# Sharing one load of second-half query weights between chunks 0 and 1, keeping the pool weights, and asking chunks 2 and 3 one pass earlier

## The chip, the cores and the metric

The kernel runs on one core of a Trainium2 chip. The metric is the time of one execution on the device, in microseconds (us). Before the change it is 2883.5 us, the median of three runs (2882.57 to 2884.82).

## What is computed

The input x holds 512 tokens of width 1024. Two layers are applied to it. Layer 0 mixes tokens with four moving averages (the "pool"), layer 1 with an attention over a compressed key-value memory. After the mixer each layer has a retrieval stage (PEER), which is most of the work:

```python
q = (h @ w_q).reshape(B, S, 8, 2, 128)             # 8 heads, two query halves each
s = einsum('bshpc,hpnc->bshpn', q, sub_keys)       # against 128 keys per half
top_s, top_i = top_k(s, 16)                        # 16 best keys of each half
best_s, pos = top_k(all 16 x 16 sums, 16)          # 16 best pairs of each head
gate = softmax(best_s)
a = einsum('tkd,td->tk', u[idx], h)                # 128 expert rows per token
x = x + einsum('tk,tkd->td', gate * gelu(a), v[idx])
```

A last stage adds x + sigmoid(norm(x) @ ple_wg) * (p @ ple_wp). All data are float32. A token wants 8 heads x 16 = 128 experts in each layer, and the rows u and v of an expert stand side by side in memory (8 KB).

## The kernel before

**Chunks, passes, gathers.** The 512 tokens are four chunks of 128. A chunk in a layer is a pair g (0 to 3 in layer 0, 4 to 7 in layer 1). Pass g runs over the 128 experts of pair g. For each expert k one indirect DMA, a gather, fetches 128 rows of 8 KB (1 MB) into one of 9 slots. There are 1024 gathers. The queue of POOL (GpSimd) issues them (line 582), and each waits until the addition of the gather nine places before has freed its slot. DVE takes the dot product of u and h (line 1648), ACT makes gelu, weight and a diagonal matrix (lines 1150 to 1158), and then either PE adds v into the accumulator in PSUM by two products with that diagonal matrix (line 933), or DVE adds it into X (line 1639). `on_dve(n)` decides which: `ADDS_ON_DVE` gives the number of additions on DVE in each pass, spread evenly over it. PE can run ahead by no more than the 5 diagonal matrices.

**Everything else happens between gathers.** A stage is a generator on each engine and is cut into parts. `STEPS[g]` lists the stages of pass g in order, and `placed_parts(g)` sets the gather before which each part begins: parts have shares (`PARTS`), and they are laid out in proportion over gathers 2 to 110 of the pass, as if there were at least 165 shares (`PACE`). In pass 0 they are laid out from gather 13. `BESIDE[g]` holds the rank stages that run beside them. Each engine works in order, so a part that waits holds up all additions and dot products behind it.

**The stages that matter here.**
- `pool` (a norm, a transposing product, a scaling into `TP`, a product with `pool_w`, a scaling into SD, an addition into X), for chunk 0 at the start and for chunks 1 to 3 in pass 0.
- `fnorm` normalises up to two chunks and puts their transposes into the halves of `TT`.
- `asks0` and `asks1` are the queries and key scores of heads 0 to 3 and 4 to 7. Each uses four pieces of `w_q` of 1 MB (pieces 0 to 3, and 4 to 7), and for each piece and chunk DVE finds the 16 best of two rows of scores (`top16`).
- `rank0` and `rank1` make expert numbers and gates of four heads. In pass 0 the first heads have stages of their own, `rank_a`, `rank_b`, `rank_c`. A gather whose k begins a new group of heads waits for their numbers.

**Which pass does what.** Chunk 0 is asked at the start (`asks0`) and in pass 0 (`asks1`). Chunk 1 has `asks0` in pass 0 and `asks1` in pass 1. Chunks 2 and 3 go together: `asks0` in pass 1, `asks1` in pass 2, in front of the embedding of chunks 0 and 1 and the keys and values of layer 1.

**Where weights stand.** SP's queue loads all pieces, in the order of `PIECES`. A piece goes to a ring of two buffers (`RING`) as soon as the piece two places before it has been used. The five pieces of the start (`pool_w` and `w_q` 0 to 3) lie in gather slots 4 to 8. `KEPT` pieces go into the key-value memory KV, which layer 0 doesn't need: `w_q` 0 to 3, loaded once for chunk 1 and used again for chunks 2 and 3. That load waits until the pool stage is over, since the pool works in KV:

```python
if where == "KV" and not there and i == 0:
    next_ffn = NC + 2 if name == "ple_wg" else g0
    sp.wait_ge(x_ready, before("x_ready", "fnorm", next_ffn))
```

Of the kernel before, what the change touches and what calls it, by code (L numbers as in the profile page):

```python
# [25 lines left out]
P = 128  # L26
S, D, DEPTH = 512, 1024, 2
NC = S // P
# [25 lines left out]
ADDS_ON_DVE = (32, 28, 32, 44, 32, 42, 26, 64)  # L54
# [46 lines left out]
RANKS = {"rank0": (0, 4), "rank1": (4, 4), "rank_a": (0, 1), "rank_b": (1, 1), "rank_c": (2, 2)}  # L101


def ranks_of(g):

    names = ("rank_a", "rank_b", "rank_c", "rank1") if g == 0 else ("rank0", "rank1")
    return {RANKS[name][0] * TOPK: name for name in names}

# [29 lines left out]
def attention(g0):  # L138
# [52 lines left out]
    "rank_c": lambda g, n: [5, 5],  # L191
    "residual": lambda g, n: [2, 0],
# [57 lines left out]
PLACE = {g0 + i: i for s, g0, n in SCHEDULE if s == "fnorm" for i in range(n)}  # L250
# [19 lines left out]
FIRST_SLOT = SLOTS - FIRST_PIECES  # L270

KEPT = [("wq", (1, 2)), ("ple_wg", (4, 6, 7))]


def homes():


    found, ringed, first = [], [], {}
    for (name, g0, i), n in PIECES.items():
        kept = [(k, groups) for k, (kept_name, groups) in enumerate(KEPT)  # L280
                if name == kept_name and g0 in groups and i < 4]
        if n < FIRST_PIECES:
            found.append(("slot", FIRST_SLOT + n, 0, None, False))
        elif kept:
            k, groups = kept[0]
            found.append(("KV", i, k, None, g0 != groups[0]))
        else:
# [13 lines left out]
         (8, "main", "asks0", 5), (10, "beside", "rank_c", 0), (13, "beside", "rank_c", 1)]  # L301


def placed_parts(g):

    placed, done = [[] for _ in range(KSEL)], 0
# [5 lines left out]
    total = max(PACE * last, sum(sum(PARTS[st[0]](*st[1:])) for st in STEPS[g]))  # L312
    for st in STEPS[g]:
        for part, share in enumerate(PARTS[st[0]](*st[1:])):
            placed[begin + int(done * (last - begin) / total)].append(("main", st, part))
            done += share
    beside = [(st, part) for st in BESIDE[g] if st[0] not in ("rank_b", "rank_c") for part in range(len(PARTS[st[0]](*st[1:])))]
    for i, (st, part) in enumerate(beside):
        first = 2 + max(u for u in range(KSEL) if any(s[0] == "asks1" for _, s, _ in placed[u]))
        at = first + 8 * i if i < 2 else first + 18 + (i - 2) * (last - 10 - first - 18) // 3  # L320
        placed[at].append(("beside", st, part))
# [55 lines left out]
def trunk(nc, consts, pools, gcols, gains, positions, x, pT, uv, weights, keys, out):  # L377
    ctx = ExitStack()
    with ctx:
# [79 lines left out]
        TP = TT[:, :, P:2 * P]  # L459
# [62 lines left out]
        def _(sp):  # L522
# [5 lines left out]
            for (name, g0, i), n in PIECES.items():  # L528
# [38 lines left out]
        def _(pool):  # L567

            nc.gpsimd.memset(rooted[:], 1.0).then_inc(one_ready, 1)
            for g in range(PAIRS):  # L570
                for k in range(KSEL):
# [3 lines left out]
                    if n < SLOTS:  # L575
                        if s >= FIRST_SLOT:
                            pool.wait_ge(weights_used, s - FIRST_SLOT + 1)
# [11 lines left out]
        def _(pe):  # L589
# [35 lines left out]
            def pool_stage(g0, n):  # L625
                for i in range(n):
# [22 lines left out]
                    for wnd in range(len(WINDOWS)):  # L649
                        for k in range(2):  # L650
                            last = nc.tensor.matmul(M[:, wnd * GW:(wnd + 1) * GW], TP[:, 2 * wnd + k, :],
# [20 lines left out]
            def asks_stage(half, g0, n):  # L672

                stage, width = f"asks{half}", n * P

# [1080 lines left out]
```

## Time and profile before

| What | Value |
|---|---|
| Median of three runs | 2883.5 us |
| The profiled execution | 2884.08 us |
| Its span, first to last instruction | 2882.3 us |
| Mean granted TensorE clock | 0.912 of full |
| PE / DVE / ACT / POOL busy | 79% / 74% / 37% / 45% |
| Moved by DMA | 1175.37 MB, mean 408 GB/s |
| Gathers' share of it | 1073.81 MB |

The span is what the profile covers. 1.8 us of the execution lie around it. Busy shares are of the span. A matmul's end is modelled, so a busy PE is not a PE at its limit. The DMA figures come from the packets of the core's 16 DMA engines.

### The profile page before, as it was taken

Reading aid. Unit: us, or ns where it says so; the run is one execution under the profiler, and the core shown is the slowest. Engines: PE = TensorE matmul, PEld = TensorE weight load, DVE = VectorE, ACT = ScalarE, POOL = GpSimd, SP = SyncE. Lnnn points to the kernel's source line nnn. Section 1 sums busy time; section 2 is a strip of 40 time slices with the busy share of each in tenths; the row PEclk is TensorE's granted clock in tenths of the full one; section 3 lists DMA queues with packets and bytes.
Section 4 is the critical chain, followed back from the end, with each engine's and each line's share of the span. In section 5 each row is a group of like instructions: output and inputs, shape, how many; then the busy total and the mean of one; then the engine's idle time right before and its main releaser. Section 6 shows DMA issues by size and latency. Waiting matters only on the chain.

```text
span 2882.3 us, 23329 instructions
## 1 busy us (share of the span) xinstructions
PE 2265.8 (79%) x6572; PEld 1170.4 (41%) x6572; DVE 2143.5 (74%) x4489; ACT 1072.4 (37%) x3181; POOL 1282.7 (45%) x1029
## 2 busy tenths in 40 slices
PE   6787667976978987888687898799967788666555
PEld 4444234522534553455253455346624433222112
DVE  6888768875797667757979766686696977677776
ACT  2443324333334333632323434364332334333222
POOL 2353543544434544533543443454444334555552
PEclk9899988988999998999898999999988999887877
DMA  9999999999999999999999999999999999999995
GB/s 363 420 399 420 419 421 401 417 420 420 419 408 412 380 420 420 419 420 420 408 420 384 416 374 419 421 419 420 420 398 420 419 420 420 420 420 420 420 421 216
DMA packets 164786, 1175.37 MB, mean 408 GB/s; under 512 B 18480, under 2 KB 19888, under 8 KB 23600
## 3 DMA queue, kind: packets, MB, share of 16 engines
q0 software_dynamic: 147456, 1073.81, 90.3%
q1 hardware_dynamic: 16624, 98.24, 8.4%
q10 hardware_dynamic: 576, 1.84, 0.2%
q8 instruction: 52, 0.85, 0.1%
q14 instruction: 78, 0.64, 0.1%
HBM read 1171.71 MB, written 2.10 MB: 407 GB/s over the span
## 4 chain that ended last, share of the span: by engine, by line
PE 36%; DMA 35%; DVE 18%; ACT 5%; issue 4%; POOL 2%; DVEq 0%; SPq 0%; ACTq 0%; POOLq 0%
DMA slot<-in_uv,idx 35%; PE acc L933 18%; DVE slot L1648 6%; DVE X L1639 3%; PE B L687 3%; PE B L605 3%; PE M L605 2%; POOL slot L582 2%; PE M L875 2%; PE M L687 1%; PE B L875 1%; ACT diag L1158 1%; DVE SD L1275 1%; DVE top_u L1280 1%; ACT A L948 1%
## 5 line engine op out<-in xcount | busy, mean ns | idle before, releaser
L933 PE MATMUL acc<-slot,diag 128*128 128x512 f32 x2904 | 1550.7, 673 | 580.9 <-ACT diag L1158 580.1
L582 POOL DMA_INDIRECT slot<-in_uv,idx x1024 | 1282.4, 1252 | 1555.3 <-PE acc L933 1076.4
L1648 DVE CUSTOM_DVE_ANT_0 slot<-slot,HP 128x1024 f32<-128x1024 f32 x1024 | 1243.3, 1221 | 564.2 <-DMA slot<-in_uv,idx 554.4
L933 PEld LDWEIGHTS acc<-slot,diag 128*128 128x128 f32 x2904 | 571.5, 210 | 1413.0 <-ACT diag L1158 853.7
L1150 ACT ACTIVATE act_a<-a 128x1 f32<-128x1 f32 x1024 | 206.6, 202 | 1616.7 <-DVE a L1648 1615.7
L1639 DVE SCALAR_TENSOR_TENSOR X<-slot,w,X 128x1024 f32<-128x1024 f32 x297 | 380.7, 1282 | 33.4 <-ACT w L1152 33.2
L1152 ACT ACTIVATE w<-act_a,gate 128x1 f32<-128x1 f32 x1024 | 301.5, 294 | 33.2
L1158 ACT ACTIVATE diag<-cst,w 128x128 f32<-128x128 f32 x726 | 291.7, 402 | 23.8
L687 PE MATMUL B<-TT,w 128*128 128x256 f32 (+1 forms) x448 | 88.8, 354 | 0.0
L687 PE MATMUL M<-TT,w 128*128 128x256 f32 (+1 forms) x448 | 88.3, 352 | 0.0
L687 PEld LDWEIGHTS B<-TT,w 128*128 128x128 f32 x448 | 78.3, 196 | 20.7 <-issue 13.1
L687 PEld LDWEIGHTS M<-TT,w 128*128 128x128 f32 x448 | 77.3, 194 | 19.4 <-issue 12.0
L1648 DVE DVE_READ_ACCUMULATOR2_ANT a<- 128x1 f32 x1024 | 84.3, 82 | 0.0
L1150 ACT ACT_TABLE_LOAD x56 | 71.8, 1283 | 12.3 <-DVE a L1648 9.4
L605 PE MATMUL M<-w,TT 128*128 128x256 f32 x272 | 61.6, 379 | 0.0
L605 PE MATMUL B<-w,TT 128*128 128x256 f32 x272 | 61.6, 379 | 0.0
L605 PEld LDWEIGHTS M<-w,TT 128*128 128x128 f32 x272 | 51.7, 190 | 14.7 <-issue 8.6
L605 PEld LDWEIGHTS B<-w,TT 128*128 128x128 f32 x272 | 51.7, 190 | 10.9 <-issue 4.3
L1273 DVE MAX8 top<-T 128x8 f32<-128x128 f32 x128 | 37.6, 294 | 15.9 <-PE T L702 15.7
L875 PE MATMUL M<-KV,TT 128*128 128x512 f32 x96 | 43.7, 603 | 0.0
L1278 DVE MAX8 top<-SD 128x8 f32<-128x128 f32 x128 | 37.8, 295 | 4.4
L702 PEld LDWEIGHTS T<-TU,A 128*128 128x128 f32 x256 | 34.4, 191 | 16.2 <-issue 14.6
(203 smaller groups left out, 1553.5 us busy)
## 6 DMA issues: line engine op xcount, KB each, us to landing
w<-in_wq SPq DMA_DIRECT2D x28, 1024.0 KB, 9.1
slot<-in_uv,idx POOLq DMA_INDIRECT x1024, 16.9
w<-in_ple_wg SPq DMA_DIRECT2D x8, 1024.0 KB, 9.1
w<-in_w_o SPq DMA_DIRECT2D x8, 1024.0 KB, 9.1
w<-in_w_dq SPq DMA_DIRECT2D x6, 1024.0 KB, 6.9
w<-in_w_uq_nope SPq DMA_DIRECT2D x8, 768.0 KB, 8.6
w<-in_ple_wp SPq DMA_DIRECT2D x5, 1024.0 KB, 14.2
slot<-in_wq SPq DMA_DIRECT2D x4, 1024.0 KB, 15.2
```

What stands on the lines that cost most here:

```text
L582: nc.gpsimd.indirect_dma_start(out=slot[s][:], out_offset=None, in_=uv[g // NC], in_offset=bass.IndirectOffsetOnAxis(ap=idx[:, g % HPB, k: ...
L605: last = nc.tensor.matmul(dst, lhsT[:, k, i * P:(i + 1) * P], wp[:, k * cols:(k + 1) * cols], start=(k == 0), stop=(k == kb - 1))
L687: last = nc.tensor.matmul(dst[:, e * 512:e * 512 + width], wp[:, k * 256 + e * P:k * 256 + (e + 1) * P], TT[:, k, 0:width], start=(k == 0) ...
L875: last = nc.tensor.matmul(MB[ch][:, half * 512:half * 512 + 512], TT[:, k0 + k, ch * P:(ch + 1) * P], wp[:, k * 512:k * 512 + 512], start= ...
L933: last = nc.tensor.matmul(acc[:, half * 512:half * 512 + 512], diag[adds_on_pe(n) % DIAGS][:], slot[s][:, D + half * 512:D + half * 512 + ...
L1150: nc.scalar.activation(act_a[:, s:s + 1], a[:, s:s + 1], ACT.Gelu_apprx_tanh).then_inc(gelued, 1)
L1152: nc.scalar.activation(w[:, s:s + 1], act_a[:, s:s + 1], ACT.Copy, scale=gate[:, g % HPB, k:k + 1]).then_inc(weighted, 1)
L1158: nc.scalar.activation(diag[adds_on_pe(n) % DIAGS][:], ident, ACT.Copy, scale=w[:, s:s + 1]).then_inc(diag_ready, 1)
L1273: step(nc.vector.max(tops[:, 0:8], values))
L1278: step(nc.vector.max(tops[:, 8:16], left))
L1639: nc.vector.scalar_tensor_tensor(Xc, slot[s][:, D:2 * D], w[:, s:s + 1], Xc, ALU.mult, ALU.add).then_inc(dve_added, 1)
L1648: nc.vector.tensor_tensor_reduce(out=slot[s][:, 0:D], in0=slot[s][:, 0:D], in1=HP[:, g % HPB, :], scale=1.0, scalar=0.0, op0=ALU.mult, op1 ...
```

## The change

Three things are changed.

1. `asks1` of chunks 0 and 1 is one stage in pass 0, `asks1 (0, 2)`, which loads `w_q` 4 to 7 once for both. For it chunk 1 goes through `pool` and `fnorm` first, so that both transposes stand in `TT`; `place_of` fixes which half. Chunk 0's ranking of heads 4 to 7 is cut in two (`rank_d`, `rank_e`). The parts of these stages are laid out over gathers 13 to 55 (`ASKED`), and the rest of the pass's parts over 55 to 110.
2. `pool_w` goes to the fourth quarter of KV and is loaded once for all chunks. `TP`, into which the pool writes, moves from `TT` to SD.
3. Chunks 2 and 3 have `asks1` in pass 1, behind their `asks0`. Pass 2 keeps the embedding, the keys and values, and the ranking of chunk 3. `trig` moves from pass 0 to pass 1, and `rank1` of chunk 2 from pass 2 to pass 1.

With it, the additions on DVE are given for each quarter of a pass: 28 in pass 0 (32 before), 22 in pass 1 (28), 43 in pass 2 (32), and as many as before in the others.

```diff
-ADDS_ON_DVE = (32, 28, 32, 44, 32, 42, 26, 64)
+QUARTER = KSEL // 4
+ADDS_ON_DVE = ((4, 4, 9, 11), (7, 5, 5, 5), (10, 6, 11, 11), (11, 11, 11, 11),
+               (8, 8, 8, 8), (10, 11, 10, 11), (7, 6, 7, 6), (16, 16, 16, 16))
...
-    spread, of = ADDS_ON_DVE[g] - DVE_HEAD, KSEL - DVE_HEAD
-    return (k - DVE_HEAD) * spread // of != (k - DVE_HEAD + 1) * spread // of
+    q, j = divmod(k, QUARTER)
+    head = DVE_HEAD if q == 0 else 0
+    spread, of = ADDS_ON_DVE[g][q] - (head if g else 0), QUARTER - head
+    return (j - head) * spread // of != (j - head + 1) * spread // of
...
 STEPS = [
-    (ask_second(0, 1) + stages_of(["pool"], 1, 3) + ask_first(1, 1) +
-     stages_of(["trig"], 0, 1)),
-    residual(0) + ask_second(1, 1) + ask_first(2, 2),
-    residual(1) + ask_second(2, 2) + stages_of(["renorm"], 3, 1) + embed(0, 2) + keys_values(4),
+    (stages_of(["pool", "fnorm"], 1, 1) + ask_second(0, 2) + stages_of(["rank_e"], 0, 1) +
+     stages_of(["pool"], 2, 2) +
+     stages_of(["asks0"], 1, 1) + rank(1, 0)),
+    residual(0) + rank(1, 1) + ask_first(2, 2) + ask_second(2, 2) + rank(2, 1) + stages_of(["trig"], 0, 1),
+    residual(1) + stages_of(["renorm"], 3, 1) + embed(0, 2) + keys_values(4),
...
 BESIDE = [
-    stages_of(["rank_b", "rank_c"], 0, 1) + rank(0, 1),
-    rank(1, 1),
-    rank(2, 1) + rank(3, 0) + rank(3, 1),
+    stages_of(["rank_b", "rank_c", "rank_d"], 0, 1),
+    [],
+    rank(3, 0) + rank(3, 1),
...
-FIRST_SLOT = SLOTS - FIRST_PIECES
-KEPT = [("wq", (1, 2)), ("ple_wg", (4, 6, 7))]
+FIRST_SLOT = SLOTS - FIRST_PIECES + 1
+POOL_HOME = 3
+KEPT = [("pool_w", (0, 1, 2)), ("wq", (1, 2)), ("ple_wg", (4, 6, 7))]
...
+ASKED = 55
...
+    for sts, end, pace in ((STEPS[g][:3], ASKED, 0), (STEPS[g][3:], last, 0)) if g == 0 else ((STEPS[g], last, PACE),):
+        done, total = 0, max(pace * last, sum(sum(PARTS[st[0]](*st[1:])) for st in sts))
...
+        if g == 0:
+            at = (ASKED - 8, ASKED - 5)[i]
+        elif g == 2:
+            at = 20 + i * (last - 30) // 3
...
-        TP = TT[:, :, P:2 * P]
+        SDH = SD[:, :].rearrange("p (a d) -> p a d", a=2)
+        scaled, TP = SDH[:, :, 0:D // 2], SDH[:, :, D // 2:D]
...
-                if where == "KV" and not there and i == 0:
-                    next_ffn = NC + 2 if name == "ple_wg" else g0
-                    sp.wait_ge(x_ready, before("x_ready", "fnorm", next_ffn))
+                if where == "KV" and not there and i == 0 and g0:
+                    free_at = ("fnorm", NC + 2) if name == "ple_wg" else ("asks0", g0)
+                    sp.wait_ge(x_ready, before("x_ready", *free_at))
...
                 stage, width = f"asks{half}", n * P
+                lo = place_of(g0) * P
+                if (half, g0) == (0, 1):
+                    pe.wait_ge(x_ready, before("x_ready", stage, g0))
...
-                                                    TT[:, k, 0:width], start=(k == 0), stop=(k == DB - 1))
+                                                    TT[:, k, lo:lo + width], start=(k == 0), stop=(k == DB - 1))
```

## Rows read from the trace of the kernel before

**Rows 1.** The page: GB/s in 40 slices, and all DMA packets.

```profile
GB/s 363 420 399 420 419 421 401 417 420 420 419 408 412 380 420 420 419 420 420 408 420 384 416 374 419 421 419 420 420 398 420 419 420 420 420 420 420 420 421 216
DMA packets 164786, 1175.37 MB, mean 408 GB/s; under 512 B 18480, under 2 KB 19888, under 8 KB 23600
```

**Rows 2.** Windows: the start, passes 0 to 6, the end; last columns clock, DMA share, GB/s.

```profile
0.00:42.80 42.80, 23.91 (x160) 21.84 (x160) 17.41 (x61) 7.00 (x13) 4.79 (x10) 0.96 0.84 324
42.80:391.60 348.80, 267.91 (x872) 140.33 (x873) 274.22 (x647) 132.66 (x397) 162.70 (x132) 0.91 1.01 416
391.60:726.20 334.60, 261.36 (x718) 129.46 (x717) 252.31 (x581) 119.40 (x380) 154.91 (x129) 0.89 1.01 415
726.20:1101.10 374.90, 327.42 (x979) 180.35 (x978) 277.65 (x608) 140.98 (x407) 166.63 (x129) 0.94 1.00 408
1101.10:1451.60 350.50, 277.55 (x867) 152.55 (x866) 266.29 (x538) 143.31 (x419) 157.47 (x129) 0.93 1.01 417
1451.60:1830.50 378.90, 323.10 (x980) 178.26 (x979) 277.69 (x608) 140.57 (x407) 158.01 (x129) 0.95 0.99 403
1830.50:2182.00 351.50, 300.78 (x1002) 168.26 (x1001) 267.14 (x536) 150.09 (x421) 159.51 (x129) 0.94 1.01 415
2182.00:2530.70 348.70, 274.20 (x659) 124.00 (x657) 260.56 (x574) 129.71 (x391) 150.86 (x129) 0.93 1.01 420
...
2842.00:2882.30 40.30, 22.62 (x49) 9.80 (x48) 21.15 (x33) 12.36 (x28) 0.00 (x0) 0.84 0.14 56
```

**Rows 3.** DMA issues of weights: count, KB each, median us to landing.

```profile
w<-in_wq SPq DMA_DIRECT2D x28, 1024.0 KB, 9.1
...
KV<-in_wq SPq DMA_DIRECT2D x4, 1024.0 KB, 16.1
...
w<-in_pool_w SPq DMA_DIRECT2D x1, 1024.0 KB, 8.9
```

**Rows 4.** Windows in passes 2 and 4, in which DMA falls short.

```profile
920.00:956.00 36.00, 32.94 (x129) 21.65 (x129) 26.74 (x56) 16.59 (x49) 18.90 (x10) 0.95 0.85 326
...
948.00:956.00 8.00, 8.00 (x28) 4.96 (x27) 5.49 (x11) 5.43 (x16) 7.39 (x3) 1.00 0.35 121
...
1664.00:1688.00 24.00, 21.53 (x67) 12.75 (x68) 18.63 (x33) 10.12 (x32) 16.87 (x9) 0.93 0.77 299
```

**Rows 5.** POOL's timeline from 941 us: gathers 335 and 336.

```profile
944.78 9.07 POOL L582 DMA_INDIRECT slot<-in_uv,idx  x1 [1.44 <-PE acc L933]
954.16 0.94 POOL L582 DMA_INDIRECT slot<-in_uv,idx  x1 [0.30 <-issue]
```

**Rows 6.** The page: all gathers of POOL; busy, mean ns, idle before, releaser.

```profile
L582 POOL DMA_INDIRECT slot<-in_uv,idx x1024 | 1282.4, 1252 | 1555.3 <-PE acc L933 1076.4
```

**Rows 7.** DVE's timeline beside it: seven dot products and an addition, first and last.

```profile
943.77 1.20 DVE L1648 CUSTOM_DVE_ANT_0 slot<-slot,HP 128x1024 f32<-128x1024 f32 x1
...
951.83 1.21 DVE L1648 CUSTOM_DVE_ANT_0 slot<-slot,HP 128x1024 f32<-128x1024 f32 x1
```

**Rows 8.** Window of gathers 16 to 39 of pass 2.

```profile
770.00:847.00 77.00, 61.13 (x174) 30.57 (x173) 71.18 (x207) 28.84 (x81) 32.88 (x25) 0.91 1.01 409
```

**Rows 9.** DVE's timeline in pass 2: a top16, a dot, an addition, the next top16.

```profile
796.12 0.28 DVE L1273 MAX8 top<-T 128x8 f32<-128x128 f32 x1
...
797.71 1.21 DVE L1648 CUSTOM_DVE_ANT_0 slot<-slot,HP 128x1024 f32<-128x1024 f32 x1
...
798.84 1.28 DVE L1639 SCALAR_TENSOR_TENSOR X<-slot,w,X 128x1024 f32<-128x1024 f32 x1
800.04 0.29 DVE L1273 MAX8 top<-T 128x8 f32<-128x128 f32 x1
```

**Rows 10.** PE's timeline: half a query piece for two chunks, one addition.

```profile
760.13 3.62 PE L687 MATMUL B<-TT,w 128*128 128x256 f32 x16
763.59 1.88 PE L933 MATMUL acc<-slot,diag 128*128 128x512 f32 x4
```

**Rows 11.** PE's timeline in pass 7: one addition, begun after a wait.

```profile
2684.70 3.66 PE L933 MATMUL acc<-slot,diag 128*128 128x512 f32 x4 [3.00 <-ACT diag L1158]
```

More of the change, by code:

```diff
@@ L191 @@
     "rank_c": lambda g, n: [5, 5],
+    "rank_d": lambda g, n: [5, 5],
+    "rank_e": lambda g, n: [5, 5],
     "residual": lambda g, n: [2, 0],
@@ L248, with place_of, asked_in @@
     t == "latent" for t, _, _ in SCHEDULE[max([0] + [j for j in range(i) if SCHEDULE[j][0] == "asks0"]):i]))]
-PLACE = {g0 + i: i for s, g0, n in SCHEDULE if s == "fnorm" for i in range(n)}
+def place_of(g):
+    return g % GROUP
+def asked_in(half, g):
+    return g if g == 0 or (g == 1 and half == 0) else g - g % GROUP
 def before(name, stage, g0):
@@ L269 @@
 FIRST_PIECES = sum(len(ids) for st in START for _, ids in USES.get(st[0], []))
-FIRST_SLOT = SLOTS - FIRST_PIECES
-KEPT = [("wq", (1, 2)), ("ple_wg", (4, 6, 7))]
+FIRST_SLOT = SLOTS - FIRST_PIECES + 1
+POOL_HOME = 3
+KEPT = [("pool_w", (0, 1, 2)), ("wq", (1, 2)), ("ple_wg", (4, 6, 7))]
 def homes():
-    found, ringed, first = [], [], {}
+    found, ringed, loads = [], [], [0] * 4
     for (name, g0, i), n in PIECES.items():
[L280 to L286, printed above, removed]
+        kept = [groups for kept_name, groups in KEPT if name == kept_name and g0 in groups and i < 4]
+        if kept:
+            home, there = POOL_HOME if name == "pool_w" else i, g0 != kept[0][0]
+            loads[home] += not there
+            found.append(("KV", home, loads[home] - 1, None, there))
+        elif n < FIRST_PIECES:
+            found.append(("slot", FIRST_SLOT + n - 1, 0, None, False))
         else:
@@ L301 @@
          (8, "main", "asks0", 5), (10, "beside", "rank_c", 0), (13, "beside", "rank_c", 1)]
+ASKED = 55
 def placed_parts(g):
-    placed, done = [[] for _ in range(KSEL)], 0
+    placed = [[] for _ in range(KSEL)]
     begin, last = DVE_HEAD - 1, KSEL - 18
@@ L311, in placed_parts @@
             placed[at].append((lane, (name, 0, 1), part))
[L312 to L316, printed above, removed]
+    for sts, end, pace in ((STEPS[g][:3], ASKED, 0), (STEPS[g][3:], last, 0)) if g == 0 else ((STEPS[g], last, PACE),):
+        done, total = 0, max(pace * last, sum(sum(PARTS[st[0]](*st[1:])) for st in sts))
+        for st in sts:
+            for part, share in enumerate(PARTS[st[0]](*st[1:])):
+                placed[begin + int(done * (end - begin) / total)].append(("main", st, part))
+                done += share
+        begin = end
     beside = [(st, part) for st in BESIDE[g] if st[0] not in ("rank_b", "rank_c") for part in range(len(PARTS[st[0]](*st[1:])))]
     for i, (st, part) in enumerate(beside):
-        first = 2 + max(u for u in range(KSEL) if any(s[0] == "asks1" for _, s, _ in placed[u]))
-        at = first + 8 * i if i < 2 else first + 18 + (i - 2) * (last - 10 - first - 18) // 3
+        if g == 0:
+            at = (ASKED - 8, ASKED - 5)[i]
+        elif g == 2:
+            at = 20 + i * (last - 30) // 3
+        else:
+            first = 2 + max(u for u in range(KSEL) if any(s[0] == "asks1" for _, s, _ in placed[u]))
+            at = first + 8 * i if i < 2 else first + 18 + (i - 2) * (last - 10 - first - 18) // 3
         placed[at].append(("beside", st, part))
@@ L576, in _ @@
                         if s >= FIRST_SLOT:
[L577 removed]
+                            pool.wait_ge(weights_used, s - FIRST_SLOT + 2)
                     elif on_dve(n - SLOTS):
@@ L1140, in _ @@
                           rank_c=lambda g, n: rank_stage("rank_c", g, n),
+                          rank_d=lambda g, n: rank_stage("rank_d", g, n),
+                          rank_e=lambda g, n: rank_stage("rank_e", g, n),
                           latent=latent_stage, keys=keys_stage, dq=dq_stage, uq=uq_stage, uqp=uqp_stage,
@@ L1282, in asks_stage @@
             def asks_stage(half, g0, n):
-                stage = f"asks{half}"
+                stage, first = f"asks{half}", place_of(g0)
                 yield
@@ L1625, in _ @@
                           rank_c=lambda g, n: rank_stage("rank_c", g, n),
+                          rank_d=lambda g, n: rank_stage("rank_d", g, n),
+                          rank_e=lambda g, n: rank_stage("rank_e", g, n),
                           latent=latent_stage, dq=dq_stage, uqp=uqp_stage, heads=heads_stage, wo=wo_stage,
```

35 lines of the change are left out of this document (22 added, 13 removed).

## The prediction

> **What bounds the kernel now.** I read the page first. In 27 of the 40 slices DMA moves 419 to 421 GB/s, and it never moves more [rows 1]. Over a whole pass it can hold that: pass 6 shows 420 [rows 2]. A gather is 1.0486 MB, so at this rate one costs 2.50 us, and the 1175.37 MB [rows 1] cost 2798.5 us of the span's 2882.3. The other 83.8 us are time in which DMA was short. POOL's waits for a freed slot [rows 6] fit: the ring of 9 slots is full most of the time.
>
> The second view is the table by pass, to find where DMA is short. I take a stretch's loss as its length times (420 - its GB/s) / 420 [rows 2]. The start loses 42.8 x 96/420 = 9.8 us, and the end 40.3 x 364/420 = 34.9. Passes 0 to 6 lose 3.3, 4.0, 10.7, 2.5, 15.3, 4.2 and 0 us. So bytes set the time, and a local stall counts only where it outlasts the ring. The third view is the stretch of pass 2 that loses most. From 920 to 956 us it loses 36 x 94/420 = 8.1 us, of which the last 8 us alone lose 5.7 [rows 4]. There one gather sat on POOL for 9.07 us, against a mean of 1.25, and the next followed at once with no wait for a slot [rows 5, 6]. In the same time DVE ran seven dot products and an addition without a gap [rows 7].
>
> **The bytes.** The change takes away five pieces of 1 MB. `asks1 (1, 1)` no longer loads `w_q` 4 to 7, and `pool_w` is loaded once instead of twice (its load into the ring [rows 3] goes). The first `w_q` pieces for chunks 1 to 3 are kept in KV before and after, and the ring then holds two pieces of `asks1 (2, 2)` from pass 0 on, and gets the other two in pass 1 instead of pass 2. The keys are loaded as often as before. 5 x 1.0486 = 5.24 MB at 420 GB/s are **-12.5 us**. That term has no upper bound beyond itself: if all five loads now filled time in which DMA was short anyway, it would be 0, and at most the 18.0 us lost in passes 0 to 2 could hide some of it. I take all of it, as the loads fall mostly in stretches at 420.
>
> **Pass 2.** It loses `asks1 (2, 2)` and `rank1` of chunk 2. The shares laid out over 108 gathers fall from 252 to 194. The latent stage begins at gather 44 instead of 59, and its part after the `w_dkv` products follows 6 gathers later instead of 4. DVE's burst between gathers 16 and 39 goes: there it was busy 71.2 of 77 us, and the stretch lost 77 x 11/420 = 2.0 us [rows 8]. The run of seven dots that goes with the long gather came from a backlog that DVE had built at the latent stage. With the parts wider apart the backlog shrinks. I take the loss of pass 2 from 10.7 to 3.0 us, **-7.7**, the level of passes 0 and 3 [rows 2]. The ends are -10.7 (nothing left) and 0 (all stalls return in new places). DVE gets 11 more additions (43 for 32), 11 x 1.20 = 13 us [rows 9], less than the 16 top16 (25 us) and the ranking (13) that leave.
>
> **Pass 0.** DVE's prices are from one stretch: a top16 796.12 to 797.71, 1.59 us; a dot 1.13; an addition 1.20 [rows 9]. A ranking of two heads I estimate at two top16 (3.2), four operations over 512 elements at half a dot each (2.4) and 2 us of small ones, 7.6 us. DVE's work is heaviest from gather 43 to 62 after the change: 20 dots 22.6, 3 additions 3.6, 12 top16 for heads 5 to 7 of two chunks 19.1, `rank_d` and `rank_e` 15.2, the next pool's norm 0.7, together 61 us. DMA brings 20 gathers in 50 us, and no weights fall there. So DVE falls 11 us behind. What the ring can take: 9 slots x 2.50 = 22.5 us from one issue to the next of a slot, less the 9.1 us of a lone piece to landing [rows 3], less some 4.5 us from dot to free slot (1.1 dot, about 1 on ACT, 1.7 to 2 for the addition), leaves about 9 us. So 2 us are lost. PE in the same stretch, gathers 26 to 55: `asks1 (0, 2)` is four pieces of two halves, 8 x 3.46 = 27.7 us [rows 10], and 3.6 for scores, an estimate. 26 additions on PE (28 of 32 a quarter) at 1.71 us are 45. That is 76 us against 75 of gathers and 5 of weights, so PE is full but doesn't fall behind. It saves little elsewhere. The three pools stay, one before the queries and two behind. The load of `w_q` 0 to 3 waits for the last pool addition (gather 77), and `asks0 (1, 1)` begins at 79, 5 us later. A lone piece takes 9.1 us [rows 3], so PE waits 4 us with its additions queued behind it, and ACT stops after 5 diagonal matrices. DVE goes on. DMA is full with those very loads, and 4 us are inside the ring's 9: price 0; were the ring already late, 4. `rank_d` ends at gather 55, whose slot gather 64 needs: no wait. Pass 0 goes from 3.3 to 5.3 us lost, **+2**. The ends are -3.3 and +11 (the whole backlog shows).
>
> **Pass 1.** The shares rise from 127 (laid out as 165) to 202. From gather 88 to 111 DVE has 24 dots 27.1, 4 additions 4.8, 8 top16 12.7, a ranking of four heads 13 and `trig` 5, 63 us against 60. PE from 21 to 54 has 31 us of queries and scores and 28 additions, 48: 79 us against 82. Both fit narrowly. I take 4.0 to 5.0, **+1**, between -4 and +7. SP's queue, once past `w_q` 7 of chunk 2, waits for `renorm`, now at gather 3 of pass 2. `gates` needs its first piece at 12, 9 gathers or 22 us later, against 9.1 for a load: 0.
>
> **Pass 4 and the rest.** Only the spread of additions changes. In the first quarter of pass 4 DVE has 8 instead of 9 or 10, beside the same burst as in pass 2. That saves 1 to 2 us of a loss of 15.3. I take **-1.5**, between -8 (the long gather of 1664 to 1688 us [rows 4] goes too) and +3.
>
> **The sum.** -12.5 - 7.7 + 2 + 1 - 1.5 = -18.7 us. The profiled execution took 2884.1 (span 2882.3 and 1.8 around it), so it would take 2865.4; the median before is 0.6 lower. I predict **2865 us**.
>
> **A rule weighed.** The long gather [rows 5] beside an unbroken run of DVE operations with two inputs in SBUF [rows 7] looks like POOL being kept out. The Trainium skill, "SBUF — State Buffer", section "Who interferes with whom", says that such a DVE operation contends with GpSimd instructions that read SBUF, and infers that descriptor generation isn't held by it. By that page the 9.07 us belong to POOL alone and would stay at 2871 us in all; by the rows they come with the run of dots, and go when it is broken. No run here separates the two yet.
>
> **Rivals.**
> - *The long gather stays.* It occurs at gather 79 of pass 2 and, with the same loss, of pass 4 [rows 4], 256 gathers apart. If it belongs to the gather's number or to any backlog at `latent`, 5.7 us of pass 2's gain are missing: 2871. For it: the same place twice. Against: both passes have the same order of work, so the same run of dots. Chance 0.18.
> - *The new bursts in passes 0 and 1 cost what pass 2 gives back.* DVE's 11 us and PE's full stretch show in whole: +11 and +7 instead of +3, 2880. For it: pass 4 lost 15.3 with much the same burst. Against: the same burst in pass 2 lost 2.0. Chance 0.10.
> - *More stalls go.* The long gather of pass 4 goes too and pass 2 is clean: 2856. Chance 0.10.
> - *Slower: PE at its lower clock in pass 0.* PE has 76 us of work at full clock in gathers 26 to 55. At the lower level (1.2 GHz) an addition takes 3.66 us instead of 1.88 [rows 10, 11], twice as long. If a share f of this work runs so, PE falls 76(1 + f) - 80 us behind, and what is over 9 is lost. It eats the gain of 19 from f = 0.42. Pass 0 shows a granted clock of 0.91 [rows 2], that is 0.18 of its time at the lower level, and the lower level followed PE's idle time; here PE is never idle. Chance 0.03, 2887.
> - *The loads are hidden anyway*, and only the bytes' time moves into idle DMA: about 2880 with the rest. In the chance of the second rival.
>
> **Chances and range.** The forecast has 0.59, 2860 to 2869. The range takes in the bounds of passes 0 to 2 and of pass 4: 2854 to 2877. It leaves out the slow end and most of the second rival. 0.2% is 5.8 us, about what a measurement of this kernel tells from no change: below 2877.7 is faster. Faster has 0.91, within 0.2% 0.06 (half of the second rival), slower 0.03.
>
> **What would show it.** Bytes: 1170.1 MB, with 24 + 4 loads of `w_q` by ring and slots, one of `pool_w`. Pass 2: GB/s near 417, no gather over 2 us on POOL, length near 362 us (374.9, less two `w_q` pieces or 5.0, less 7.7). Pass 1: about 331 us (two pieces fewer, +1). Pass 0: about 348 (one piece fewer, +2). The window of gathers 43 to 70 of pass 0 shows 400 to 415 GB/s. The forecast is wrong if DMA moves under 412 in pass 0 or 1, or if POOL has a long gather in any of the first three passes.

## The result and the profile after

The change makes the kernel slower: 2890.6 us (median of 12 runs, 2887.4 to 2895.3) against 2883.8 us before (12 runs, 2882.1 to 2885.3). The ratio is 1.0024, with a 95% interval of 1.0016 to 1.0032. The forecast was 2865 us, with a range of 2854 to 2877. The profiled execution has a span of 2888.1 us, 5.8 more than before.

The page of the changed kernel, its GB/s in 40 slices and its packets, answers to [rows 1].

```profile
GB/s 371 387 378 379 419 420 411 399 419 386 420 419 382 420 419 420 419 420 420 405 420 386 416 376 420 420 420 419 420 404 420 419 420 416 420 420 420 420 420 216
...
DMA packets 164065, 1170.11 MB, mean 405 GB/s; under 512 B 18400, under 2 KB 19808, under 8 KB 23520
```

The bytes are as forecast: 1170.1 MB, with 24 loads of `w_q` into the ring and one of `pool_w`. But the mean rate fell from 408 to 405 GB/s, and slices 2 to 4 (72 to 289 us, pass 0) show 378 to 387 where the kernel before had 399 to 420. The table by pass answers to [rows 2]: the start, passes 0 to 5.

```profile
0.00:41.30 41.30, 22.33 (x160) 20.76 (x160) 17.43 (x62) 7.00 (x13) 4.80 (x10) 0.92 0.86 336
41.30:403.50 362.20, 281.85 (x880) 151.13 (x880) 282.33 (x707) 136.75 (x401) 163.49 (x132) 0.91 0.98 397
403.50:738.60 335.10, 274.12 (x760) 140.35 (x760) 272.36 (x709) 127.39 (x392) 149.99 (x129) 0.93 1.00 406
738.60:1107.80 369.20, 298.56 (x801) 151.23 (x802) 249.98 (x437) 134.04 (x394) 165.42 (x129) 0.90 1.00 412
1107.80:1457.70 349.90, 281.97 (x859) 155.05 (x858) 265.82 (x538) 143.22 (x419) 155.94 (x128) 0.90 1.01 417
1457.70:1837.10 379.40, 327.23 (x985) 181.08 (x984) 277.80 (x609) 140.79 (x407) 162.53 (x129) 0.94 0.99 404
1837.10:2188.10 351.00, 300.11 (x996) 167.34 (x995) 267.56 (x536) 149.58 (x421) 165.95 (x128) 0.93 1.01 417
```

By the same formula, length times (420 - GB/s) / 420, the losses are:

| Pass | Lost before, us | Forecast | Lost after | Length before, forecast, after |
|---|---|---|---|---|
| 0 | 3.3 | 5.3 | 19.8 | 348.8, 348, 362.2 |
| 1 | 4.0 | 5.0 | 11.2 | 334.6, 331, 335.1 |
| 2 | 10.7 | 3.0 | 7.0 | 374.9, 362, 369.2 |
| 4 | 15.3 | 13.8 | 14.5 | 378.9, -, 379.4 |

Passes 0 and 1 lose 23.7 us more, the start and passes 2, 4 and 5 some 7.7 less, and the bytes give 12.5. That gives 3.5 of the span's 5.8 us. Pass 6 and the end lose 1 us more than before, and a row's GB/s are whole numbers, which is up to 0.4 us for each pass.

Two counts that the forecast went by have to be set right. The four numbers of `ADDS_ON_DVE` for pass 2 add up to 38 additions on DVE, not 43: 39 begin in the window of pass 2 above, 33 in that of the kernel before. And pass 0 had 29 of them before, not 32, since its first three additions go to PE; it has 28 now. In the first half of pass 0 they fall from 14 to 8, so the change itself gave PE six additions more there.

Where the losses stand is seen in finer windows of the changed kernel. By the dot products in them they are gathers 17 to 34 and 49 to 69 of pass 0, 33 to 48 and 104 to 118 of pass 1, and 53 to 67 of pass 2.

```profile
92.00:136.00 44.00, 39.54 (x116) 21.72 (x115) 30.93 (x49) 18.94 (x58) 18.68 (x15) 0.92 0.94 366
...
180.00:244.00 64.00, 48.05 (x136) 23.61 (x135) 57.43 (x171) 31.29 (x77) 25.32 (x22) 0.87 0.88 329
484.00:532.00 48.00, 47.51 (x168) 28.81 (x166) 39.13 (x128) 14.85 (x49) 20.43 (x20) 1.00 0.98 377
680.00:712.00 32.00, 23.73 (x47) 9.69 (x47) 28.03 (x60) 14.68 (x45) 17.83 (x13) 0.89 0.89 341
896.00:936.00 40.00, 36.76 (x139) 23.59 (x138) 24.69 (x51) 17.11 (x51) 21.43 (x12) 0.96 0.91 351
```

They lose 5.7, 13.9, 4.9, 6.0 and 6.6 us. In the second DVE is busy 57.4 of 64 us: that is the burst that the forecast had counted. In the first PE is busy 39.5 of 44 us. The waits from 88 to 136 us (who waited for whom, total us, times, longest) show POOL behind PE, first in the changed kernel, then in the kernel before:

```profile
POOL slot L606 <- PE acc L961: 34.9, 11, 8.3
...
POOL slot L582 <- PE acc L933: 22.6, 11, 2.6
```

The long gather of pass 2 did not go. POOL's timeline answers to [rows 5]: gather 322 (number 66 of pass 2) and gather 591 (number 79 of pass 4) with the one behind it.

```profile
918.52 8.06 POOL L606 DMA_INDIRECT slot<-in_uv,idx  x1 [0.31 <-issue]
...
1680.21 11.41 POOL L606 DMA_INDIRECT slot<-in_uv,idx  x1 [1.44 <-PE acc L961]
1691.93 0.94 POOL L606 DMA_INDIRECT slot<-in_uv,idx  x1 [0.30 <-issue]
```

### The profile page after: what moved, and what is told of

Its sections match the earlier page's. It is cut to its first block, busy times and chain, and to the rows that moved or that the text cites. A ratio compares the mean times of both kernels' runs of the same rounds, so it can differ in the third digit from the quotient of the medians.

```text
span 2888.1 us, 23092 instructions
## 1 busy us (share of the span) xinstructions
PE 2271.9 (79%) x6448; PEld 1167.4 (40%) x6448; DVE 2144.2 (74%) x4505; ACT 1077.4 (37%) x3184; POOL 1287.0 (45%) x1029
## 4 chain that ended last, share of the span: by engine, by line
PE 38%; DMA 31%; DVE 19%; ACT 5%; issue 5%; POOL 2%; DVEq 0%; SPq 0%; ACTq 0%; POOLq 0%
DMA slot<-in_uv,idx 31%; PE acc L961 20%; DVE slot L1687 7%; PE B L715 3%; DVE X L1678 3%; PE M L629 2%; PE B L629 2%; POOL slot L606 2%; PE M L715 2%; PE M L903 1%; ACT diag L1189 1%; PE B L903 1%; DVE top_u L1316 1%; ACT w L1183 1%; DVE SD L1311 1%
## 5 line engine op out<-in xcount | busy, mean ns | idle before, releaser
L961 PEld LDWEIGHTS acc<-slot,diag 128*128 128x128 f32 x2908 | 577.8, 211 | 1417.9 <-ACT diag L1189 825.3
L715 PE MATMUL B<-TT,w 128*128 128x256 f32 x384 | 87.1, 382 | 0.0
L715 PE MATMUL M<-TT,w 128*128 128x256 f32 x384 | 86.1, 379 | 0.0
L1687 DVE DVE_READ_ACCUMULATOR2_ANT a<- 128x1 f32 x1024 | 83.8, 82 | 0.0
## 6 DMA issues: line engine op xcount, KB each, us to landing
w<-in_ple_wp SPq DMA_DIRECT2D x5, 1024.0 KB, 13.6
```

The costliest lines, as they stand in the source:

```text
L715: last = nc.tensor.matmul(dst[:, e * 512:e * 512 + width], wp[:, k * 256 + e * P:k * 256 + (e + 1) * P], TT[:, k, lo:lo + width], start=(k ...
L961: last = nc.tensor.matmul(acc[:, half * 512:half * 512 + 512], diag[adds_on_pe(n) % DIAGS][:], slot[s][:, D + half * 512:D + half * 512 + ...
L1687: nc.vector.tensor_tensor_reduce(out=slot[s][:, 0:D], in0=slot[s][:, 0:D], in1=HP[:, g % HPB, :], scale=1.0, scalar=0.0, op0=ALU.mult, op1 ...
```

## The experiments

Ratios are against the kernel before, whose median was 2883.3 to 2884.9 us beside them. Losses are by the formula above, from each kernel's own window of the pass, and each kernel has one profile. Two profiles of the same instructions differ: pass 0 is the same in the kernel with `trig` moved and in that with `trig` moved and gaps in passes 2 and 4 (both below), and took 362.3 us in one and 358.8 in the other. So the length or the loss of a pass is good to some 3 or 4 us, and what a change is worth is read from the medians.

### Pass 1: `trig`

```diff
-    residual(0) + ... + ask_second(2, 2) + rank(2, 1) + stages_of(["trig"], 0, 1),
-    residual(1) + stages_of(["renorm"], 3, 1) + embed(0, 2) + keys_values(4),
+    residual(0) + ... + ask_second(2, 2) + rank(2, 1),
+    residual(1) + stages_of(["renorm"], 3, 1) + stages_of(["trig"], 0, 1) + embed(0, 2) + keys_values(4),
```

> The changed kernel with trig moved from the end of pass 1 into pass 2, behind renorm. Theory A: pass 1 ends with a ranking of four heads and then 6.2 us of trig in one piece (685.9 to 692.1 us in its trace) on DVE while slots have been waiting 8 us already; this empties the ring, and 32 x 79/420 = 6.0 us are lost from 680 to 712 us. Then pass 1 loses 5 us less and pass 2, in which DVE has room, nothing more: about 2885. Theory B: the stretch is short because DVE as a whole has too much in gathers 88 to 106, whatever stands last: the loss falls by 1 to 2 us, about 2889.

Measured: 2879.1 us, ratio 0.9982 (0.9972 to 0.9991). 11.5 us less than the changed kernel, for one small stage. Its windows of passes 1 and 2:

```profile
405.30:735.60 330.30, 270.57 (x760) 139.17 (x760) 268.40 (x687) 125.03 (x389) 149.78 (x129) 0.94 1.01 417
735.60:1101.40 365.80, 293.11 (x794) 148.96 (x795) 255.62 (x459) 134.59 (x395) 155.77 (x128) 0.93 1.00 412
```

Pass 1 loses 2.4 us instead of 11.2 and is 4.8 us shorter. Pass 2 loses 7.0 us, as in the changed kernel, and is 3.4 us shorter, since some 1.4 MB less is moved in it and 1.7 MB more in pass 1. Theory A holds, and more was gained than it asked. DVE's timeline of the changed kernel shows the piece, from the last dot before `trig` to the next:

```profile
684.75 1.21 DVE L1687 CUSTOM_DVE_ANT_0 slot<-slot,HP 128x1024 f32<-128x1024 f32 x1
...
686.62 0.16 DVE L1416 CAST pos_f<-pos_i 128x4 f32<-128x4 int32 x1
...
692.05 0.23 DVE L1443 TENSOR_SCALAR cs<-cs 128x128 f32<-128x128 f32 x1
692.19 1.22 DVE L1687 CUSTOM_DVE_ANT_0 slot<-slot,HP 128x1024 f32<-128x1024 f32 x1
```

`trig` is only 5.6 us of it, but with the end of the ranking before it no dot begins for 7.4 us, and the slots were already late: gathers 97 to 104 of the pass had stood loaded for 7.6 to 8.7 us when their dots began.

Not all of the 8.8 us less lost is the end of the pass. 6.0 stood there, and 2.5 in gathers 33 to 48, where nothing was changed. The profiled execution (2883.6 us) was the slowest of ten.

### Pass 0: DVE's burst

```diff
                     for r in range(2 * n):
+                        if (half, g0) == (1, 0) and r >= 2:
+                            settle()
+                            step(nc.vector.tensor_copy(top[:, 1, 4 + p, r % 2, :], top[:, 0, 4 + p, r % 2, :]))
+                            found = nc.vector.tensor_copy(top_u[:, 1, 4 + p, r % 2, :], top_u[:, 0, 4 + p, r % 2, :])
...
+                            continue
                         found = top16(T[:, j * 512 + r * P:j * 512 + (r + 1) * P],
```

> The changed kernel, in which chunk 1 isn't searched in the shared second-half stage of pass 0: its eight top16 (1.6 us each) are replaced by copies of chunk 0's results (leaves out part of the computation: chunk 1 gets chunk 0's places for heads 4 to 7; the gathers are as many and as large). Theory A: the loss of 64 x 91/420 = 13.9 us from 180 to 244 us is DVE's burst of 61 us in the time of 50 us of gathers; with some 10 us of it gone, the loss there falls to 4 us or less, about 2880. Theory B: PE, whose queries for two chunks stand beside 28 of 32 additions in each quarter, sets it: the loss stays above 9 us, 2887 or more.

Measured: 2884.6 us, ratio 0.9999 (0.9989 to 1.0009). This is 6.0 us less than the changed kernel, so it lies between the two theories' numbers. The window of pass 0:

```profile
41.30:397.50 356.20, 278.95 (x880) 150.06 (x880) 272.24 (x658) 136.99 (x401) 163.40 (x132) 0.92 0.99 404
```

The pass loses 13.6 us instead of 19.8. DVE is busy 10 us less, and 6 us show in the length of the pass as in the medians. The burst is part of the cause, but the pass still loses 10 us more than before the change.

### What a byte is worth here

```diff
+                if (name, g0, i) == ("wq", 1, 0):
+                    for again in range(4):
+                        r = again % 2
+                        sp.wait_ge(weights_used, PIECES["wq", 0, 6 + r] + 1)
...
+                        sp.dma_start(ring[HOMES[PIECES["wq", 0, 6 + r]][1]][:], weights["wq", 0][4 + again]
+                                     ).then_inc(spare_loaded[r], 16)
```

> The changed kernel with 4 MB of loads more (four w_q pieces loaded once more into the ring in pass 0, after its last pieces were used, and read by nobody). Theory A: the saved bytes were worth 2.5 us each only where DMA is full; here they fall into gathers 43 to 70 of pass 0, where it isn't, and the time rises by at most 4 us, to 2890 to 2895. Theory B: bytes cost 2.5 us each wherever they are, since a gather that waits behind them is late in turn: 2901.

Measured: 2891.0 us, ratio 1.0021 (1.0010 to 1.0032). Four MB more cost 0.4 us, within the scatter. Theory A holds. The window from 180 to 244 us shows where they went:

```profile
180.00:244.00 64.00, 47.93 (x133) 22.95 (x132) 57.34 (x178) 30.81 (x77) 23.80 (x21) 0.87 0.97 393
```

It has 393 GB/s instead of 329 with the engines equally busy. This tells what a byte is worth in that stretch. It does not tell what the saved ones were worth: by the bytes of the windows one of them is missing in pass 0, three in pass 1 and one in pass 2.

> The kernel before with the pool weights kept in KV alone: one load of 1 MB fewer, and hardly another instruction changed. The load that goes lands between gathers 16 and 32 of pass 0, where DMA is full. Theory A: a byte saved where DMA is full is worth its 2.5 us per MB: 2881. Theory B: the wait that ends the next stall in pass 0 (35 to 52) takes it back: 2883.5.

This is the other half of the question, the kernel before with `pool_w` kept in KV and nothing else:

```diff
-KEPT = [("wq", (1, 2)), ("ple_wg", (4, 6, 7))]
+KEPT = [("pool_w", (0, 1)), ("wq", (1, 2)), ("ple_wg", (4, 6, 7))]
```

Measured: 2881.2 us, ratio 0.9992 (0.9983 to 1.0001). The medians differ by the expected 2.5 us, but the interval just takes in no change. With DMA full a MB is worth its 2.5 us as far as this can tell; in the stretch where the engines bind, 4 MB were worth 0.4 us.

### The long gathers

```diff
                 dve.wait_ge(rows_loaded[s], 16 * (n // SLOTS + 1))
+                if n:
+                    dve.wait_ge(dotted, n)
```

> The changed kernel, in which every dot product first waits for the end of the one before it, so that DVE never runs dot products back to back without a gap. Theory A: the long gathers on POOL (8.06 us at gather 322 and 11.41 us at gather 591) are POOL kept out by a run of DVE operations without a gap; with gaps no gather is on POOL for more than about 2.5 us, and the two losses go: 6 to 10 us, about 2882. Theory B: they are POOL's own, by the gather's number or by its queue: they stay, at the same or other gathers, and the time doesn't change.

Measured: 2890.4 us, ratio 1.0026 (1.0016 to 1.0035), no faster. But of all 1024 gathers none is on POOL for more than 2.14 us. POOL's line in the changed kernel, then in this one, as min/median/max in ns:

```profile
L606 POOL DMA_INDIRECT slot<-in_uv,idx x1024: 932/948/11412, 35.6 to 2843.5; - x171
```

```profile
L606 POOL DMA_INDIRECT slot<-in_uv,idx x1024: 932/968/2142, 37.6 to 2839.1; - x171
```

So it is shown that the long gathers come with DVE's run without gaps, as theory A has it, but its time is not: pass 4 is 374.8 us instead of 379.4, but passes 3 and 6 are 2.0 and 1.4 us longer, and no gain is left in the medians. The next kernels have the gap only where long gathers had been:

```diff
                 dve.wait_ge(rows_loaded[s], 16 * (n // SLOTS + 1))
+                if g in (2, 4) and 56 <= k < 84:
+                    dve.wait_ge(dotted, n)
```

> The changed kernel with trig in pass 2, and with the wait for the dot before only for gathers 56 to 83 of passes 2 and 4. Theory A: the gaps take away the long gathers (11.42 us at gather 591, and what is left of the one near 322) at no cost elsewhere: pass 4 loses 9.5 us or less instead of 13.1, and the time is 2874 to 2876. Theory B: the long gather only takes the place of another wait, since the ring is empty there in any case: 2879.

> The version with trig in pass 2 and ten additions on DVE in the first quarter of pass 0, with the wait for the dot before in gathers 56 to 83 of passes 2 and 4. If the long gather's 3 to 4 us of pass 4 come on top: 2872 to 2873. If the gap's gain was a chance of one profile: 2876.

The first of the two is the kernel with `trig` moved and these gaps: 2878.5 us, ratio 0.9979 (0.9970 to 0.9988). That is 0.6 us below its sister without gaps, a miss for theory A, though pass 4 loses 9.8 us instead of 13.5 in the profile. The profiled execution, 2874.6 us, was one of its fastest. The second has six early additions more (see the next section): 2868.0 us, ratio 0.9947 (0.9933 to 0.9961), 7.9 us below its sister. The pairs had run on different occasions, so the larger one was run again, side by side, together with the kernel before with nothing but the gaps.

> The version with trig in pass 2 and ten additions on DVE in the first quarter of pass 0, a second time, as the neighbour of the next: 2876.

> The same with the wait for the dot before in gathers 56 to 83 of passes 2 and 4, side by side with it. Theory A: the long gather of pass 4 costs what the profiles show, 13.6 against 7.0 us lost there: 4 to 8 us faster than its neighbour, 2868 to 2872. Theory B: the ring is empty there in any case: the same time.

> The kernel before with that wait alone, in gathers 56 to 83 of passes 2 and 4. Theory A: both long gathers (9.07 and 9.08 us, 5 to 6 us lost with each) go, and the time falls by 7 to 11 us: 2873 to 2877. Theory B: the gaps cost DVE as much or the losses stay under another name: 2884.

Measured: 2875.7 us (ratio 0.9969, 0.9958 to 0.9981), 2870.3 us (0.9949, 0.9935 to 0.9963), and 2877.2 us (0.9974, 0.9963 to 0.9984). The kernel before gains 7.7 us by the gaps alone. Its windows of passes 2, 4 and 5, with the rows between left out:

```profile
729.20:1100.10 370.90, 322.53 (x980) 178.63 (x979) 277.52 (x608) 140.41 (x407) 156.32 (x129) 0.95 1.01 413
...
1451.60:1824.10 372.50, 323.26 (x983) 179.25 (x982) 278.15 (x609) 140.25 (x407) 150.84 (x129) 0.96 1.00 410
1824.10:2180.80 356.70, 305.95 (x998) 168.93 (x997) 267.25 (x535) 150.01 (x421) 159.69 (x129) 0.91 1.00 410
```

Passes 2 and 4 are 4.0 and 6.4 us shorter than in [rows 2], and pass 5, in which nothing was changed, 5.2 us longer in this one profile. The profiled execution (2881.05 us) was the slowest of the eight, and the median is 3.9 us below it. So a long gather costs some 4 to 6 us where it stands, and part of it can come back later.

### Pass 0: PE's backlog

```diff
-ADDS_ON_DVE = ((4, 4, 9, 11), ...
+ADDS_ON_DVE = ((10, 4, 9, 11), ...
```

> The changed kernel with trig in pass 2 (2879 us by the run before) and six additions more on DVE in the first quarter of pass 0 (10 instead of 4). Theory A: the 6 us lost between gathers 16 and 35 of pass 0 are PE's backlog: slots are held 15 to 18 us after their dot, beside queries for two chunks and 28 of 32 additions on PE, while DVE is busy only 12 of 18 us. With fewer additions on PE the slots are held some 5 us shorter, and 3 to 5 us of the loss go: 2875. Theory B: PE waits there for DVE's parts (the pool's scalings stand between rankings), so more work on DVE makes it no better or worse: 2879 to 2883.

The first half of pass 0 has 14 additions on DVE with this, as many as before the change. Measured: 2875.9 us, ratio 0.9976 (0.9965 to 0.9987), and 2875.7 when run again. By the medians that is 3.2 us less than with `trig` moved alone; the intervals of the two ratios overlap. The time is the one that theory A named, and below the 2879 to 2883 of theory B. POOL's wait for PE from 90 to 138 us is down from 34.9 us in 11 waits (88 to 136 us of the changed kernel) to:

```profile
POOL slot L606 <- PE acc L961: 23.1, 8, 7.0
```

The pass loses 12.7 us instead of 19.8. Not only the early loss shrinks: the one between gathers 40 and 75, where the additions are unchanged, goes from 14.3 to 9.1 us. With the six additions it is 9.1 to 9.9 us in four profiles, without them 12.8 to 14.3 in four (and 11.5 with a gap before every dot). So DVE's burst began with the ring already late, because of PE.

A part of the early loss is PE's clock. PE waits there for ACT's diagonal matrix, and the eight products behind that wait ran slower in the changed kernel than in the kernel with `trig` moved and the gaps, whose pass 0 is the same. The changed kernel comes first, then the other:

```profile
110.50 6.72 PE L961 MATMUL acc<-slot,diag 128*128 128x512 f32 x8 [2.94 <-ACT diag L1189]
...
112.58 3.70 PE L961 MATMUL acc<-slot,diag 128*128 128x512 f32 x8 [2.94 <-ACT diag L1189]
```

For them the clock was at the lower of its two levels, 1.2 GHz instead of 2.4. The granted clock and the GB/s of the stretch go with it: a window of 6.5 us at the eight products, and of the 44 us around them in the other kernel (0.92 and 366 GB/s in the changed kernel, above):

```profile
110.50:117.00 6.50, 6.50 (x8) 2.67 (x9) 6.50 (x12) 1.91 (x8) 1.72 (x1) 0.53 0.84 339
...
94.00:138.00 44.00, 39.53 (x128) 22.67 (x127) 31.44 (x50) 19.39 (x58) 21.47 (x17) 1.00 0.99 395
```

The 3.0 us fall where POOL waits for PE. From the issue of gather 16 to that of 40, 5.6 to 7.3 us are lost in the five profiles with the lower clock and 4 additions on DVE, 2.7 and 4.2 in the two at the upper clock (the second has a gap before every dot), and 2.6 to 3.7 in the six with 10 additions, at the lower clock for most of these products (5.6 to 6.0 us for eight). Why the clock differed is open; no run was made to hold it.

> The version with trig in pass 2 and ten additions on DVE in the first quarter of pass 0 (2875.9 us by the run before, 12.9 us lost in pass 0), and chunk 1 not searched in the shared stage of pass 0, as in the run with half of the top16 (leaves out that part of the computation: chunk 1 gets chunk 0's places for heads 4 to 7). Theory A: pass 0 loses by two separate causes, PE's backlog of gathers 16 to 35 and DVE's burst of gathers 43 to 62. Each alone took away 6 to 7 us, so together they leave 6 to 7 of 20, near the 3.7 of the kernel before, and the time is about 2870. Theory B: both act on the same slack of the ring and together give little more than one: 12 us lost in pass 0, 2875.

Both together: 2869.9 us, ratio 0.9950 (0.9935 to 0.9965). The window of pass 0:

```profile
42.80:393.50 350.70, 269.21 (x856) 145.56 (x856) 279.45 (x664) 134.74 (x395) 157.61 (x131) 0.91 1.00 410
```

It loses 8.4 us. Separate causes were to leave 6 to 7, one slack 12. In the profiles PE's backlog and DVE's burst each stand for 4 to 7 us of pass 0, by the medians for 3.2 and 6.0, and they add up (2879.1 to 2869.9 us for both). Of the 16.5 us that pass 0 lost more, 5 are left. They stand from gather 26 on and from 56 on, near the pools on either side of the queries. That the pools are their cause is argued from these places only; no run took them away.

> The same with one addition on DVE instead of four in gathers 32 to 63 of pass 0, which takes 3.6 us out of DVE's burst and gives PE 5 us more. If DVE's burst alone sets the loss there: 2 to 3 us faster than its neighbour, 2870. If PE is as full: no gain or slower.

With three additions fewer on DVE in the second quarter (`(10, 1, 9, 11)`): 2869.9 us (2866.1 to 2873.1) beside 2868.0 (2866.2 to 2870.0). No gain. That PE is as full there is argued; the run shows only that taking these additions from DVE does not help.

### The parts one by one

```diff
-    residual(0) + rank(1, 1) + ask_first(2, 2) + ask_second(2, 2) + rank(2, 1) + stages_of(["trig"], 0, 1),
-    residual(1) + stages_of(["renorm"], 3, 1) + embed(0, 2) + keys_values(4),
+    residual(0) + rank(1, 1) + ask_first(2, 2) + stages_of(["trig"], 0, 1),
+    residual(1) + ask_second(2, 2) + stages_of(["renorm"], 3, 1) + embed(0, 2) + keys_values(4),
```

> The changed kernel without its third part: chunks 2 and 3 have their second half in pass 2 as before, with rank1 of chunk 2 there and as many additions on DVE in passes 1 and 2 as before; trig stands at the end of the lighter pass 1. Theory A: the shared load alone costs its 16 us of loss in pass 0 and saves 12.5 in bytes, and passes 1 and 2 lose what they lost before (3.6 and 10.4): about 2886. Theory B: pass 1 loses by trig whatever stands before it: 2890.

The additions on DVE in passes 1 and 2 are as many as before the change here, and `rank1` of chunk 2 is back in pass 2. Measured: 2884.4 us, ratio 1.0003 (0.9994 to 1.0013), with the windows of passes 0 to 2:

```profile
41.40:403.90 362.50, 282.35 (x880) 151.44 (x880) 282.35 (x706) 136.68 (x401) 161.90 (x132) 0.90 0.98 396
403.90:728.00 324.10, 242.14 (x583) 109.99 (x584) 245.47 (x537) 121.00 (x379) 155.16 (x129) 0.91 1.01 418
728.00:1105.70 377.70, 327.79 (x980) 181.76 (x979) 277.55 (x609) 140.47 (x407) 162.35 (x129) 0.94 0.99 405
```

The first two parts keep their whole loss in pass 0 (20.7 us), pass 1 falls to 1.5, although `trig` stands at its end here too, and pass 2 has 13.5. So `trig` costs only behind a full pass, and the first two parts together, the shared load and the kept pool weights, come out even. The third part took it from there to 2890.6; with `trig` in pass 2 the same three parts run at 2879.1, which is 5.3 us below the first two.

> The kernel before with the third part alone: chunks 2 and 3 have their second half in pass 1 (behind chunk 1's own second half and its ranking), rank1 of chunk 2 goes with them, pass 2 is laid out as in the changed kernel, and trig stays in pass 0. No byte is saved. Theory A: moving work out of pass 2 gains what pass 2 lost more than other passes, 4 us, and pass 1, full to 225 shares, loses as much or more: 2883 to 2890. Theory B: pass 2's relief is real and pass 1 has room: 2878 to 2880.

The third part alone, on the kernel before:

```diff
-    residual(0) + ask_second(1, 1) + ask_first(2, 2),
-    residual(1) + ask_second(2, 2) + stages_of(["renorm"], 3, 1) + ...
+    residual(0) + ask_second(1, 1) + rank(1, 1) + ask_first(2, 2) + ask_second(2, 2) + rank(2, 1),
+    residual(1) + stages_of(["renorm"], 3, 1) + ...
```

Here the ranking in pass 2 is laid out as in the changed kernel, no addition is moved, and pass 1 holds chunk 1's own second half as well. Measured: 2890.6 us, ratio 1.0026 (1.0015 to 1.0036), 0.6 us above the range of theory A. Pass 1:

```profile
392.90:741.60 348.70, 280.28 (x870) 150.25 (x868) 285.65 (x757) 124.15 (x387) 151.18 (x129) 0.94 0.99 403
```

It loses 14.1 us instead of 4.0, while pass 2 loses 7.0 instead of 10.7.

## Why the prediction was wrong

- **The bytes (-12.5).** Five MB did go. What each was worth depended on the place. The prediction took all of it "as the loads fall mostly in stretches at 420", and it priced the bytes at 420 and new losses apart from them. That sum is not wrong as a sum, but the losses grew by 18.3 us (102.1 us of the span against 83.8), past what the bytes gave. Where DMA is short, bytes are worth nothing: 4 MB put into the late stretch of pass 0 left the time the same.
- **Pass 0 (+2, measured +16.5).** This is the step that failed: the loss of pass 0, priced at 2 us, from a slack of 9 us that the ring did not have. DVE's work of gathers 43 to 62 was forecast at 61 us. The changed kernel's dots of gathers 43 and 63 begin at 166.8 and 228.9 us, 62 us apart. But "the ring can take" 9 us was worked out for a full ring, and the ring was not full: PE's queue had used it up. The prediction found PE with 76 us of work in 80 and called this "full but doesn't fall behind". It took the two engines' margins one by one, though both draw on the same nine slots. The runs show it: six additions moved from PE to DVE a pass-quarter earlier took some 3 to 5 us from the later loss as well. The backlog began ahead of the gathers 26 to 55 that were summed: at gathers 23 to 25 PE waited 2.94 us for ACT and then worked at the lower clock, which took 3.0 us. From 120 to 180 us PE was indeed "never idle" (59.94 of 60 us, granted clock 1.00). It also counted no wait of one engine for another inside the pool stage. DVE stood there 4.5 us for ACT's norm and 3.9 us for PE's transposing product, with the dot products behind it. In size the runs account for 11.4 of the 16.5 us (19.8 to 8.4 with both causes lowered); the last 5 stay open.

DVE's timeline in the changed kernel, the two waits:

```profile
81.09 0.16 DVE L1214 RECIPROCAL rstd<-rms 128x1 f32<-128x1 f32 x1 [4.47 <-ACT rms L979]
...
92.30 1.23 DVE L1234 TENSOR_TENSOR SD<-T,gc 128x1024 f32<-128x1024 f32 x1 [3.89 <-PE T L663]
```

- **Pass 1 (+1, measured +7.2).** The sum of DVE's work in gathers 88 to 111, 63 us against 60, was close: those gathers took 66 us (634 to 700). What failed was the step from there to a loss of 1 us, which looked at the sum and not at its form. A stage in parts lets a dot through after each top16; `trig` does not. Its 5.6 us came when slots were already 8 us late, and no slot came free in time: POOL issued gathers at 689.27 and then at 698.53 us. Moving it removed 11.5 us of time, and the 6.0 us lost at that place. Gathers 33 to 48 lost 4.9 us besides, with PE busy 47.5 of 48 us, and 2.4 with `trig` moved: "fit narrowly" was not met there either.
- **Pass 2 (-7.7, measured -3.7).** The rival "the long gather stays" came true, as did the condition it was given: the latent stage moved from gather 59 to 44, and the long gather from 79 to 66, behind a new backlog. It needs DVE's run without gaps and doesn't go by the gather's number: it moved, and went with gaps. The forecast erred in holding that wider parts would break the run. The relief of the burst at gathers 16 to 39 did come (0.2 us lost there). And the forecast gave DVE 11 additions more, where it got 6: the other five stayed with PE, which was busy 36.8 of 40 us where the pass lost 6.6. No run tried another number.
- **Pass 4 (-1.5, measured -0.8).** The small gain was right, though the long gather grew from 9.08 to 11.41 us: the addition now falls one dot earlier, and the run is longer by an addition and a dot.
- **The load of `w_q` 0 to 3 behind the pools, SP's wait for `renorm`, `rank_d`: 0.** Right. From gather 76 of pass 0 on nothing is lost.
- **The rivals.** The likeliest was the second, that the new bursts show in whole; it gave 2880 with +18 for the two passes, and they came to +23.7. It had 0.10 and deserved the most; and the 0.91 for "faster" counted half of it in, though its own 2880 lies above the 2877.7 named as the bound. The slower side was put on PE's clock alone. That rival came true in small: it wanted the lower clock for 0.42 of the work, the granted clock of pass 0 is 0.91 before and after, and the one stretch found cost PE 3.0 us, and pass 0 some 3 us. It does not explain the slowdown.
- **The rule weighed.** The Trainium skill, "SBUF — State Buffer", "Who interferes with whom", infers that a DVE operation with two SBUF inputs does not hold descriptor generation. The measurements decide against it for this case: with DVE's dots apart, the longest of 1024 gathers is 2.14 us instead of 11.41, and in the kernel before 1.99 instead of 9.08. That the shared port is what is held was not shown. The lock that the Trainium skill describes there is for one instruction. Here six to nine of them began while one gather was held, and each of the four long ones of the two kernels ended 0.8 us after DVE fell idle (926.58 after 925.77 us in the first of the changed kernel).

The forecast's gain exists. The kernel with all three parts, `trig` in pass 2, six early additions on DVE and the gaps runs at 2868.0 and 2870.3 us in two trials, 0.9947 and 0.9949 of the kernel before. It beats both kernels. Not all of the gain is the three parts': the gaps alone gave the kernel before 7.7 us.

## What to carry to other kernels

In a kernel whose transfers are full, count saved bytes only after asking which engine binds in the stretch that is to be shortened; put the bytes back there, and if the time stays, they were free. Slack in a ring is one account for all engines behind it: add their overruns and their waits for each other, and look at how long slots are held at the start of a burst, not at a full ring. Cut every stage that stands in a late stretch into pieces, the small ones too.

## What was not expected of the hardware

- A gather issued by POOL can be held there as long as DVE runs dots and additions without a gap: 8.06 to 11.53 us, against a median of 0.95, and 3.36 us where two dots followed, with `trig` in pass 2. It needs more than a run: the changed kernel has one of 12 operations (1420 to 1434 us) in which each gather passes within 2 us. What starts the long one is open.
- A wait of DVE for its own last dot is enough to let POOL in, and cost nothing measurable where it was put in two passes only.
- The same eight products behind the same wait of 2.94 us took 6.72 us in one execution and 3.70 in another, at the clock's lower and upper level, and pass 0 was 3.4 us longer in the first (362.2 and 358.8).
- The changed kernel scatters more than the kernel before (7.8 us between its fastest and slowest of 12 runs, against 3.2), as one would expect where engines take turns in binding rather than DMA, the clock with them; this is argued, not shown.
